# Output phase and experts in one block, the recurrence's output as rows, and the gather of the expert inputs ahead of the last stores

## What is computed

```python
def hybrid_mixer(h, ...):
    u, q, zf, zb, iv, g = jnp.split(h @ w_in, cuts, axis=-1)
    mixed = jnp.fft.fft2(ug, axes=(1, 3), norm="ortho").real
    y_fourier = jnp.einsum("blgc,gcd->blgd", mixed, w_fnet)
    o_fwd = chunked_gated_recurrence(qh, k_f, vh, logf_f)
    o_bwd = jnp.flip(chunked_gated_recurrence(<all flipped>), 1)
    y_rec = rms_norm(o_fwd + o_bwd, out_norm) * silu(g)
    return jnp.concatenate([y_fourier, y_rec], axis=-1) @ w_out

def expert_choice_ffn(h, w_router, w_gate, w_up, w_down):
    affinity = jax.nn.softmax(xt @ w_router, axis=-1)
    g, idx = lax.top_k(affinity.T, cap)          # tokens of each expert
    xe = xt[idx]
    he = jax.nn.silu(xe @ w_gate) * (xe @ w_up)  # per expert
    ye = (he @ w_down) * g[..., None]
    return jnp.zeros_like(xt).at[idx.reshape(-1)].add(ye.reshape(-1, d))

x = x + hybrid_mixer(rms_norm(x, norm_mix), ...)
x = x + expert_choice_ffn(rms_norm(x, norm_ffn), ...)
return rms_norm(x, norm_final)
```

## Time and profile before

| | us |
|---|---|
| time, median of 3 runs (lowest, highest) | 2569.03 (2568.76, 2569.17) |
| the profiled execution | 2567.04 |
| its span | 2565.3 |
| TensorE busy | 2523.4 |
| VectorE busy | 1641.6 |
| ScalarE busy | 1359.7 |
| GpSimd busy | 320.3 |

### The profile page before, as it was taken

The page is one execution under the profiler, slowest core; times in us unless marked ns, Lnnn a source line. Parts: engine busy times, 40 slices in busy tenths (PEclk is TensorE's granted clock), DMA queues, the critical chain, the costliest instruction groups (busy, mean ns, idle before and its releaser), DMA issues.

```text
span 2565.3 us, 45249 instructions
## 1 busy us (share of the span) xinstructions
PE 2523.4 (98%) x18541; PEld 2275.4 (89%) x18541; DVE 1641.6 (64%) x1984; ACT 1359.7 (53%) x1627; POOL 320.3 (12%) x240
## 2 busy tenths in 40 slices
PE   8999999999998999999999999999999999999998
PEld 6777777788877999999999999999999999999997
DVE  6555555435287666767666676766767666676667
ACT  6434353424655555555555555555555555555556
POOL 3102020101112011020202102021020202102010
PEclk9999999999998999999999999999999999999999
DMA  4101010135446576776767667576676767667677
GB/s 159 31 18 55 2 55 2 58 116 203 165 164 243 215 274 225 257 243 237 248 224 257 236 228 263 213 267 227 253 245 235 250 227 254 240 238 253 229 254 283
DMA packets 63991, 503.14 MB, mean 196 GB/s; under 512 B 7536, under 2 KB 7920, under 8 KB 39568
## 3 DMA queue, kind: packets, MB, share of 16 engines
q1 hardware_dynamic: 47872, 448.82, 47.9%
q0 software_dynamic: 16016, 52.85, 7.1%
HBM read 464.48 MB, written 37.22 MB: 196 GB/s over the span
## 4 chain that ended last, share of the span: by engine, by line
PE 73%; DVE 2%; ACT 1%; DMA 1%; issue 1%; POOL 0%; DVEq 0%; ACTq 0%
PE up_banks_b L2217 15%; PE up_banks_a L2217 15%; PE up_banks_b L2220 6%; PE up_banks_a L2220 6%; PE up_banks_b L2258 2%; PE up_banks_b L2256 2%; PE up_banks_b L2257 2%; PE up_banks_b L2255 2%; PE up_banks_a L2259 2%; PE up_banks_b L2259 2%; PE up_banks_a L2256 2%; PE up_banks_a L2258 2%; PE up_banks_a L2255 2%; PE up_banks_a L2257 2%; PE bank_d L65 2%; PE bank_d L66 2%
## 5 line engine op out<-in xcount | busy, mean ns | idle before, releaser
L1985 DVE TENSOR_TENSOR big_lo<-wide,big_hi 128x4096 fp32r<-128x4096 f32 x189 | 836.4, 4426 | 409.8 <-ACT big_hi L1750 409.7
L1750 ACT CAST big_hi<-wide 128x4096 fp32r<-128x4096 f32 x190 | 690.1, 3632 | 508.3 <-PE up_banks_a L2217 240.7
L2217 PE MATMUL up_banks_b<-x_parts,big_hi 128*128 128x384 f32 x2016 | 574.3, 356 | 0.0
L2217 PE MATMUL up_banks_a<-x_parts,big_hi 128*128 128x384 f32 x1984 | 565.0, 356 | 0.9 <-DVE h_parts L2009 0.9
L2220 PE MATMUL up_banks_b<-x_parts,big_lo 128*128 128x192 f32 x1764 | 442.0, 251 | 0.0
L2220 PE MATMUL up_banks_a<-x_parts,big_lo 128*128 128x192 f32 x1736 | 435.0, 251 | 0.0
L2217 PEld LDWEIGHTS up_banks_b<-x_parts,big_hi 128*128 128x128 f32 x2016 | 365.3, 189 | 0.2
L2217 PEld LDWEIGHTS up_banks_a<-x_parts,big_hi 128*128 128x128 f32 x1984 | 359.4, 189 | 1.9 <-DVE h_parts L2009 1.2
L2220 PEld LDWEIGHTS up_banks_b<-x_parts,big_lo 128*128 128x128 f32 x1764 | 336.1, 191 | 0.0
L2220 PEld LDWEIGHTS up_banks_a<-x_parts,big_lo 128*128 128x128 f32 x1736 | 330.8, 191 | 0.6
L65 PE MATMUL bank<-big_hi,w_hi 128*128 128x512 f32 x576 | 236.8, 411 | 0.0
(11 more groups left out here) (346 smaller groups left out, 4188.8 us busy)
## 6 DMA issues: line engine op xcount, KB each, us to landing
wide<-in_expert_weights SPq DMA_DIRECT2D x190, 2048.0 KB, 7.8
w_raw<-in_w_heads SPq DMA_DIRECT2D x48, 256.0 KB, 2.8
x_in<-in_x SPq DMA_DIRECT2D x12, 512.0 KB, 4.0
x_d<-in_x POOLq DMA_DIRECT2D x12, 512.0 KB, 4.7
residual<-x_d POOLq DMA_DIRECT2D x12, 512.0 KB, 3.1
ffn_in<-h_and_xT_d POOLq DMA_DIRECT2D x12, 512.0 KB, 3.1
wide<-residual SPq DMA_DIRECT2D x12, 512.0 KB, 6.5
tab<-in_tables POOLq DMA_DIRECT2D x10, 512.0 KB, 7.7
```

What stands on the lines that cost most here:

```text
L1750: nc.scalar.copy(ahead.hi(c), raw[:, c % RAW]).then_inc(hi_done, 1)
L1985: nc.vector.tensor_tensor(ahead.lo(c), raw[:, c % RAW], ahead.hi(c).bitcast(F32), ALU.subtract).then_inc(lo_done, 1)
L2217: last = nc.tensor.matmul(out[:, 0:2 * CAP], hi, x[:, k], start=n == 0, stop=n == KT - 1, skip_group_check=True)
```

## The change

1. **Recurrence as rows.** The products into `o_acc` get their operands in the other order, so that it has tokens on its partitions and the head's channels along its columns. The squares are then summed along the columns by VectorE (`reduce_sum` into `sums`); the root on ScalarE waits for that (`root`); VectorE takes the inverse and multiplies `o_acc` by it into `k_tok` (new, one instruction a block); TensorE transposes that back (`rows`, 4 transposes a block), and `out` multiplies it into `gate`. The norm weights now enter when `gate` is made. `ss` and `bc` are gone. `rows` of blocks 1 and 2 take banks of ring SC, where `bc` took MS for block 1 and SC for block 2.
2. **One block** for the output phase and the experts: no meeting of all engines between them.
3. **Space.** `x_parts` and the rows of the last norm weights lie in the space of the Fourier tables, which are done by then. ScalarE writes the squares of tiles 8 to 11 into those rows instead of `h`; the wait for `h`'s store stands ahead of the normed row there.
4. **Last tiles.** The rounds of tiles 8 to 11 are placed by hand and `PAUSES` is gone; the first half of tile 11 is added before the last two rounds, its second half after the merge; the routing of tile 10 stands before the last products; the list is turned between the two halves of `turn_rows(11)`.
5. **Gather ahead of stores.** The sample gather stands before the last store of `x`. Chunk 2 is loaded only once the gather has landed, as chunk 3.
6. **Low part of chunk 1.** Three of its four pieces on GpSimd move in between the last stores. Its high part on ScalarE is made whole at tile 9.
7. **First expert.** The prompt's list is turned after half of the third chunk's sample products instead of after the first chunk's. The sixteen idle turns stand in one piece behind the turns of the gathered rows. The low part of the sample's inputs comes one round earlier on VectorE.
8. The masks come as bytes over SyncE's queue instead of being converted by a DMA of GpSimd's; two settings on GpSimd go.

```diff
-                at_slot[f + 1] += [("ss", h, blocks[0])]
+                at_slot[f + 1] += [("root", h, blocks[0])]
                 at_slot[f + 2] += [("rstd", h, blocks[0])]
-                at_end[f + 2] += [(kind, h, b) for kind in ("bc", "out") for b in blocks]
+                at_end[f + 2] += [(kind, h, b) for kind in ("rows", "out") for b in blocks]
...
-            elif ev[0] in ("kt", "u") and ev[2] == 1 or ev[0] == "bc" and ev[2] == 2:
+            elif ev[0] in ("kt", "u") and ev[2] == 1 or ev[0] == "rows" and ev[2] >= 1:
...
-                            step(nc.vector.tensor_tensor(gate[:, n % NG], s, x, ALU.mult))
+                            step(nc.vector.scalar_tensor_tensor(out=gate[:, n % NG], in0=s, scalar=onorm[:], in1=x,
+                                                                op0=ALU.mult, op1=ALU.mult))
...
-                        nc.vector.scalar_tensor_tensor(out=g, in0=o_acc[b][:].rearrange("p c t -> p (c t)"),
-                                                       scalar=onorm[:], in1=g, op0=ALU.mult, op1=ALU.mult).then_inc(weighed, 1)
+                        nc.vector.reduce_sum(sums[:, b // 2], k_tok[:, b // 2], AX_X).then_inc(summed, 1)
...
                         nc.vector.reciprocal(rstd[:, 0:count], rms[:, 0:count]).then_inc(rstd_ready, 1)
+                        dve.wait_ge(rstd_ready, order["root"][("root", h, first)] + 1)
+                        for b in (1, 2) if first else (0,):
+                            nc.vector.tensor_tensor(k_tok[:, b // 2], o_acc[b][:],
+                                                    rstd[:, b // 2].unsqueeze(2).to_broadcast([P, CH, P]), ALU.mult).then_inc(o_scaled, 1)
...
-                            last = nc.tensor.matmul(bank[i][:, c], rstd[:, b // 2, c:c + 1].to_broadcast([P, P]), ident[:],
-                                                    start=(c == 0), stop=(c == CH - 1), skip_group_check=True)
+                            last = nc.tensor.transpose(bank[i][:, c], k_tok[:, b // 2, c], ident[:])
...
-                pool.wait_ge(added, 2 * s + 2)
-                pool.dma_start(acc[row:row + P], x[:, s % 2]).then_inc(x2_stored[s % 2], 16)
                 if t == TT:
-                    pool.wait_ge(h_stored, 16 * (TT - 1))
+                    pool.wait_ge(h_stored, 16 * S_TILES)
                     pool.wait_ge(ahead.tokens_ready, 1)
                     pool.indirect_dma_start(ahead.xs, ...)
+                pool.wait_ge(added, 2 * s + 2)
+                pool.dma_start(acc[row:row + P], x[:, s % 2]).then_inc(x2_stored[s % 2], 16)
+                for k in ahead.LOW_BETWEEN.get(s, ()):
+                    ahead.low_early(pool, nc.gpsimd, 1, slice(k, k + 2))
...
-            sp.wait_ge(filled, 2 * TT)
-            sp.dma_start(ahead.raw[:, 2], ahead.weights[0, 2]).then_inc(ahead.raw_loaded[2], 16)
...
-            for c in range(RAW, CHUNKS):
+            for c in range(ahead.EARLY, CHUNKS):
                 if c < RAW + 2:
-                    sp.wait_ge(gathered, 16 * (c - RAW + 1))
+                    sp.wait_ge(gathered, 16 * max(c - RAW + 1, 1))
```

More of the change, by code:

```diff
@@ L393, in heads_phase @@
         order = {kind: {ev: i for i, ev in enumerate(e for e in timeline if e[0] == kind)}
-                 for kind in ("update", "inter", "square", "ss", "bc")}
+                 for kind in ("update", "inter", "square", "root", "rows")}
         order_of_dir = [{ev: i for i, ev in enumerate(e for e in timeline if e[0] == "update" and e[2] == d)}
@@ L462, in _ @@
                 sp.dma_start(lb[:], lb_params).then_inc(const_loaded, 16)
[L463 removed]
+                sp.dma_start(mask[:], masks).then_inc(const_loaded, 16)
+                stores = iter([("rows",) + ev[1:] for ev in timeline if ev[0] == "out"])
                 def store(ev):
@@ L805, in _ @@
                         i = fill_of[into][0]
-                    if kind in ("begin", "level", "vt", "kt", "u", "ss", "bc") and free_at[into]:
+                    if kind in ("begin", "level", "vt", "kt", "u", "rows") and free_at[into]:
                         pe.wait_ge(bank_read[i], free_at[into])
@@ L1538, in experts_phase @@
+def experts_phase(nc, block, weights, norm_final, h_dram, acc, stored, outs, ahead):
     with ExitStack() as ctx:
@@ new lines, in _, with load_rows, store_rows @@
+        @block.sync
+        def _(sp):
+            for c in range(ahead.EARLY, CHUNKS):
+                if c < RAW + 2:
+                    sp.wait_ge(gathered, 16 * max(c - RAW + 1, 1))
+                else:
+                    sp.wait_ge(lo_done, c + 1)
+                sp.dma_start(raw[:, c % RAW], weights[0, c]).then_inc(raw_loaded[c % RAW], 16)
+            with sp.Fori(1, NE) as e:
+                for c in range(CHUNKS):
+                    sp.wait_ge(lo_done, e * CHUNKS + c + 1)
+                    sp.dma_start(raw[:, c % RAW], weights[e, c]).then_inc(raw_loaded[c % RAW], 16)
+            sp.dma_start(nw[:], norm_final.partition_broadcast(P)).then_inc(const_loaded, 16)
+            sp.wait_ge(scattered, LAST * 32)
+            def load_rows(i):
+                sp.wait_ge(lo_done, LAST * CHUNKS + CHUNKS - RAW + i + 1 + RAW)
+                for j in range(CH):
+                    t = CH * i + j
+                    if i >= 1:
+                        sp.wait_ge(rows_loaded[j], 16 * (OTHER_ROWS + i))
+                    sp.dma_start(row_tile(t), acc[t * P:(t + 1) * P]).then_inc(rows_loaded[j], 16)
+            def store_rows(tiles):
+                for t in tiles:
+                    out, row = (outs[1], t) if t < S_TILES else (outs[0], t - S_TILES)
+                    sp.wait_ge(scaled, t + 1)
+                    sp.dma_start(out[row * P:(row + 1) * P], row_tile(t)).then_inc(rows_stored, 16)
+            load_rows(0)
+            load_rows(1)
+            store_rows(range(2))
+            load_rows(2)
+            store_rows(range(2, TT))
```

2063 lines of the change are left out of this document (1015 added, 1048 removed).

## The result

| | before | after |
|---|---|---|
| median of 5 runs (lowest, highest), us | 2569.17 (2568.76, 2570.32) | 2554.93 (2554.22, 2556.18) |
| the profiled execution | 2567.04 | 2554.8 |
| its span | 2565.3 | 2553.0 |

The ratio is 0.9947 with a 95% interval from 0.9934 to 0.996: 14.2 us faster. The forecast was 2552, range 2547.5 to 2562.

What follows compares the result with a forecast made beforehand. It took TensorE to be full in the recurrence and the expert loop, with a hole of 11.5 us at the hand-over. Recurrence 12 plus hand-over 5 made 17 us, so 2552 us, range 2547.5 to 2562.

Steps and rivals of the forecast that it cites:

- (c): Recurrence, TensorE: three waits for ScalarE to empty the bank of V's transposes go, 2.5 us.
- (a): Recurrence, TensorE: the 192 products with a column of ones go, 4.6 us.
- (b): Recurrence, TensorE: 12 broadcast blocks of the inverse root become transposes, 0.55 us each, 6.6 us, or 5.6 after a deduction.
- The deduction at the end: End of the recurrence: the last two blocks' saving is lost because the block boundary waits for VectorE, 1.0 us off.
- I take nothing: Recurrence, VectorE: the 12 new scalings, 8 us, stand where it waited for level products and cost no time.
- The hand-over: From output phase to experts: earlier list turn and faster sample gather bring the work behind forward, 5 us.
- The count: First expert: 40 products stand ahead of the prompt lists' turn instead of 24, 9.4 us, 10 with a slow start.
- The clock: First expert: up to 2 us gained at 2.4 GHz and up to 2 lost behind the new 3 us wait cancel.
- B: Rival: the hand-over gives nothing, by a slow gather, a list held back by GpSimd or a grown wait; 2557, chance 0.2.
- C: Rival: the recurrence gives half, because TensorE waits for the scaled rows; 2558, chance 0.1.
- D: Rival: VectorE stands still for ScalarE's root ahead of the level steps and TensorE runs dry; 2576, chance 0.03.
- E: Rival: TensorE's freed time turns up as waits for VectorE, or work doesn't become time otherwise; 2567, chance 0.05.

Runs made afterwards that it cites:

- experiment 4: The changed kernel with VectorE making every scaling of o_acc into k_tok twice; 2562.98 us, ratio 0.9976.
- experiment 10: The changed kernel with the prompt's list turned after a quarter of the third chunk's sample products instead of half; 2554.25 us, ratio 0.9939.
- experiment 8: The changed kernel without its sixteen idle turns ahead of the first expert product; 2558.05 us, ratio 0.9964.
- experiment 6: The changed kernel with the third weight chunk loaded beside the sample's gather, as before; 2556.82 us, ratio 0.9949.
- rows-only trace: The kernel before with the whole first phase of the changed one, output phase and experts as before; 2560.85 us, ratio 0.9968.

## Why the prediction was right, step by step

**Recurrence, TensorE.** The three terms were 4.6, 6.6 (before its deduction) and 2.5, 13.7 in all. V to R, which holds all of it, became 12.5 us shorter: 500.37 and 500.39 without the rows, 487.81 to 487.91 in the ten executions with them. Of the terms only (c) was taken alone (3.2 with its bank back). The traces of before and after assign the rest. From the start of each TensorE instruction to the start of the next, summed by kind from the very first turns of V (45.97 us in the trace of before) to R:

| kind | before | after | less | forecast |
|---|---|---|---|---|
| products with ones | 4.27 | | 4.3 | 4.6 |
| level products | 40.38 | 41.22 | -0.8 | |
| broadcasts, now transposes | 11.38 | 5.60 | 5.8 | 6.6 |
| V's turns, with the wait behind them | 8.22 | 5.22 | 3.0 | 2.5 |
| all other | 455.64 | 455.42 | 0.2 | |

So (a) was too high by 1.2: the ones gave 4.3, and at seven places where they had stood between a level and a projection, the direct change from one to the other now costs 0.1 us each. (b) was too high by 0.8. Two transpose blocks stand in the 0.87 us between the rows below, the forecast's 0.43 each, but over all twelve, with the step to the work behind, a broadcast block took 0.95 and a transpose block 0.47, so 0.48 was saved and not 0.55. (c) was too low by 0.5. Together these three make 1.5 less, of which the other work gave 0.2 back: the 12.5 that were measured, to 0.1.

**The deduction at the end.** I took 1.0 off for the last two blocks, because VectorE ends the phase. It was 1.7 (R to B, 3.08 to 4.76). TensorE at that place, after:

```profile
553.88 1.03 PE L890 MATMUL bank<-ident_b,k_tok 128*128 128x128 f32 x8
554.75 1.95 PE L896 MATMUL o_acc<-fourier_space 128*128 128x128 f32 x16
559.51 0.47 PE L1408 MATMUL bank_d<-fourier_space 128*128 128x128 f32 x2 [2.81 <-PEq L455]
```

And three rows of the trace of before: ScalarE's first square behind the last state product, the first fold, and the first Fourier product:

```profile
555.28 1.09 ACT L622 ACTIVATE k_tok<-o_acc 128x512 f32<-128x512 f32 x2 [3.49 <-PE o_acc L888]
...
561.71 0.15 DVE L144 COPY fourier_space<-fourier_rows 128x1 f32<-128x1 f32 x1 [1.26 <-DMA fourier_rows<-fnet_u]
...
568.94 0.47 PE L1392 MATMUL bank_d<-fourier_space 128*128 128x128 f32 x2 [1.13 <-PEq L456]
```

The chain goes: last state product, load of the Fourier rows by SyncE, four folds on VectorE, two `out` products, stores, end of the block. From that square (after: at 545.95) to the first Fourier product it is 568.94 - 555.28 = 13.66 us before and 559.51 - 545.95 = 13.56 after. What TensorE saves behind the last state product (the last products with ones as well as the last broadcasts, 1.8 us between the two traces) is therefore worth nothing; I had left out the ones. So the recurrence gives 12.5 - 1.7 = 10.8 instead of 12.

**Recurrence, VectorE.** "I take nothing" holds for one scaling a block. That they stand in its waiting time was the right reason, but the 175 us of waiting suggested far more room than there is (experiment 4). The right reading was the time between the scaling and the place where TensorE asks for the rows, 0.3 us at three places, not the sum of waits.

**The hand-over.** 5 us forecast, 3.75 measured between these two traces (2.8 to 3.8 with their scatter). Each step, after against before, in us, with the forecast's step behind it:

| step | before | after | forecast |
|---|---|---|---|
| T to the turn of the sample's list | 141.48 | 139.52 | |
| turn of the list to the gather's issue | 1.28 | 2.05 | both together -1.7, were -1.2 |
| issue to the rows' turns | 7.76 | 4.94 | 4.3 |
| turns to the first product | 5.27 | 5.91 | 5.3 |
| first product to the prompt list's turn | 8.74 | 11.06 | 10.3 |
| that turn to the prompt rows' turns | 7.69 | 4.99 | 6 |

TensorE and the tiles:

```profile
757.04 0.23 PE L1534 MATMUL bank_d<-ident_e,table 16*128 16x16 f32 x1 [0.52 <-DVEq L1384]
...
769.94 0.47 PE L2191 MATMUL up_banks_a<-big_hi,x_parts 128*128 128x512 f32 x1 [1.09 <-DVE x_parts L2037]
...
781.00 0.32 PE L2303 MATMUL up_banks_a<-ident_e,table 48*128 48x48 f32 x2
...
785.99 0.44 PE L2179 MATMUL up_banks_a<-ident_e,wide 128*128 128x128 f32 x2 [2.64 <-DMA wide<-ffn_in,next_token]
```

The new wait of about 3 us came, with 2.6, and the gather was freed by the load's move, as said. Mis-sized were: the cast of the list, which now stands behind a half-tile addition and a softmax step on VectorE (0.8 us later); the gather, 4.9 and not 4.3; and the way to the first product, where VectorE runs a round (766.12 to 767.60) before the low parts (0.6). Against these the list's turn came out 1 us nearer to the prompt's rows.

What each edit gave of the 1.2 us up to the gather's issue (one block, the list turned between tile 11's halves, the gather ahead of the store) was not taken apart.

Two steps failed in their reason, and hid each other. The count: not 40 products stand ahead of the prompt's list but 48, two groups of sixteen, the low group of eight and half of the third chunk's sixteen. 48 x 0.23 = 11.04, and 11.06 were measured; VectorE had the list merged at 780.10, 0.9 us before TensorE came (experiment 10). The clock: I let gain and loss cancel. The gain was 2.1 us (experiment 8). The loss behind the new wait is real, but it came in six traces of ten and was 0.9 to 1.1 us there; in neither trace of the changed kernel did it come.

**Rivals.** B is out: the gather is at 4.9 us and the list isn't held back. Its load mechanism is real (experiment 6), but worth 1.3 us of the hand-over, not all of it. C and D did not occur: no wait for scaled rows. But experiment 4 shows that C was nearer than its chance of 0.1 says: one more instruction of 0.68 us a block brings the waits. E did occur in one place, the block's end, with 1.7 us.

**From work to time.** By the stretches the change is worth 12.46 - 1.68 + 3.75 = 14.5 us (13.8 with the old hand-over of the rows-only trace); the medians say 14.2, and 14.8 when the changed kernel ran again. The two profiled spans differ by 12.3 only: the profile of before began 1.35 us earlier and that of after lost 0.8 us from B to T. For the same reasons the first expert product came at 769.94, 12.0 us before 781.92, and not the 17 of the forecast's sign.

## What to carry to other kernels

TensorE's saved work counts only up to the last event from which another chain (here a load, folds and stores) leads to the end of the phase: find that event first, and price what lies behind it at nothing. The idle time of an engine in sum says nothing about the room at one place; read the gap at that place, or double the instruction. A change of a few tenths of a per cent is told by stretches between events that repeat to 0.1 us, where medians scatter by 1; but take a second trace of both kernels, since not every stretch repeats (the old hand-over: 0.8 us apart).

## What the runs showed of the hardware

GpSimd's subtraction from and into SBUF holds back one kind of VectorE instruction and not others: a TENSOR_SCALAR of 128x16 took 0.99 to 1.12 us beside it in eleven traces and 0.23 alone, while the three steps of a round (0.67 to 0.68 us each on 48x512) took the same time either way. After one and the same wait of 2.8 us TensorE's granted clock was 0.5 to 0.6 over the next 4 us in some executions and 1.00 in others, in the changed kernel 0.58 once and 1.00 once; after another wait of 2.6 to 2.7 us it fell to 0.50 in six traces of ten. So the price of such a wait has a chance part. Sixteen TensorE turns of the identity brought the clock from 0.50 back to 1.00 ahead of a stretch in which, without them, the products ran at 1.2 GHz.
